# Summing the first 80 context row tiles on VectorE in runs of 16

## The reference

```python
sc = jnp.einsum('thsk,hsnk->thsn', qp, subkeys)             # scores against 2 x 128 keys, 8 heads
top_s, top_i = lax.top_k(sc, 16)
...
best_s, best_p = lax.top_k(cand_s, 16)                      # of 16 x 16 sums
expert = jnp.take_along_axis(cand_i, best_p, axis=-1)
g = jax.nn.softmax(best_s, axis=-1)
act = jax.nn.gelu(jnp.einsum('thkd,td->thk', u_tab[expert], xt))
return jnp.einsum('thk,thkd->td', g * act, v_tab[expert])
```

## Time and profile before

| | |
|---|---|
| median of 3 runs | 4857.98 us (4857.04 to 4867.78) |
| the profiled execution | 4852.7 us, span 4851.0 us |
| TensorE (PE) busy, whole span | 3834.6 us, 79% |
| VectorE (DVE) busy | 2912.3 us, 60% |
| ScalarE (ACT) busy | 1545.0 us, 32% |
| GpSimd (POOL) busy | 1622.4 us, 33% |
| chain that ended last | PE 43%, DMA 25%, DVE 20%, issue 6%, ACT 3% |

### The profile page before, as it was taken

One profiled execution on the slowest core, in us unless ns is written; L12 is line 12 of the kernel. 1 busy time (PEld: TensorE's weight loads), 2 busy tenths in 40 slices (PEclk: granted clock), 3 DMA queues, 4 the chain that ended last, 5 costly groups with the idle time before them and its releaser, 6 DMA issues.

```text
span 4851.0 us, 43978 instructions
## 1 busy us (share of the span) xinstructions
PE 3834.6 (79%) x11761; PEld 1564.1 (32%) x11761; DVE 2912.3 (60%) x6845; ACT 1545.0 (32%) x4811; POOL 1622.4 (33%) x1312
## 2 busy tenths in 40 slices
PE   6999898889999657999876669988876656666666
PEld 4645355554444212344322113344222211111110
DVE  1112588666576697454488885455568996544544
ACT  4111244332122233333333333233433433333333
POOL 0000133222232233333333334344333425555554
PEclk8999899999999867999977679999987766666666
DMA  6544788889999887999988989999999879999998
GB/s 256 217 182 184 252 313 294 308 296 356 361 411 372 328 333 282 380 380 380 402 347 348 392 322 400 422 384 398 413 390 385 335 291 366 410 421 414 414 421 353
DMA packets 290056, 1687.27 MB, mean 348 GB/s; under 512 B 29136, under 2 KB 71184, under 8 KB 111120
## 3 DMA queue, kind: packets, MB, share of 16 engines
q0 software_dynamic: 184320, 1342.26, 69.7%
q1 hardware_dynamic: 97472, 318.79, 17.4%
q10 hardware_dynamic: 8016, 23.42, 1.5%
HBM read 1646.57 MB, written 37.78 MB: 347 GB/s over the span
## 4 chain that ended last, share of the span: by engine, by line
PE 43%; DMA 25%; DVE 20%; issue 6%; ACT 3%; POOL 1%; SPq 1%; DVEq 0%; ACTq 0%; POOLq 0%
PE ps L1218 31%; DMA slots<-in_peer,idxR 20%; PE ps L1234 8%; DVE slots L1503 6%; POOL slots L959 1%; DVE gsmR L1582 1%; DMA ring<-in_wq 1%; DVE ti L1523 1%; DVE ti L1520 1%; DMA ring<-in_mlat 1%; DVE hot L1555 1%; DVE hot L1559 1%; DVE picked L1561 1%; DVE tv L1522 1%; ACT lhs L1010 1%
## 5 line engine op out<-in xcount | busy, mean ns | idle before, releaser
L959 POOL DMA_INDIRECT slots<-in_peer,idxR x1280 | 1616.0, 1263 | 3175.3 <-PE ps L1234 2042.6
L1234 PE MATMUL ps<-slots,lhs 128*64 128x512 f32 x4544 | 1523.5, 785 | 823.5 <-ACT lhs L1010 804.2
L1503 DVE CUSTOM_DVE_ANT_0 slots<-slots,h2R 128x1024 f32<-128x1024 f32 x1280 | 1543.1, 1224 | 670.9 <-issue 591.1
L1218 PE MATMUL ps<-ring,arena 128*128 128x512 f32 (+1 forms) x3996 | 1577.7, 552 | 42.0 <-DMA ring<-in_wq 22.7
L1218 PEld LDWEIGHTS ps<-ring,arena 128*128 128x128 f32 x3996 | 764.8, 195 | 872.8 <-issue 804.6
L1234 PEld LDWEIGHTS ps<-slots,lhs 128*64 128x64 f32 x4544 | 298.0, 161 | 1943.3 <-ACT lhs L1010 1678.5
L999 ACT ACTIVATE gelus<-dots 128x1 f32<-128x1 f32 x1280 | 256.1, 200 | 1651.7 <-DVE dots L1503 1640.1
L1010 ACT ACTIVATE lhs<-fold,wgts 128x64 f32<-128x64 f32 x1136 | 395.1, 348 | 37.1
L1002 ACT ACTIVATE wgts<-gelus,gsmR 128x1 f32<-128x1 f32 x1280 | 377.1, 295 | 42.5 <-ACT gelus L999 0.5
L1218 PE MATMUL ps<-ring,slots 128*128 128x512 f32 (+1 forms) x704 | 250.7, 518 | 0.0
L1515 DVE SCALAR_TENSOR_TENSOR slots<-slots,wgts 128x1024 f32<-128x1024 f32 x135 | 173.1, 1282 | 91.1 <-ACT wgts L1002 85.5
(11 more groups left out here) (198 smaller groups left out, 2380.0 us busy)
## 6 DMA issues: line engine op xcount, KB each, us to landing
ring<-in_whead SPq DMA_DIRECT2D x24, 2048.0 KB
ring<-in_wa SPq DMA_DIRECT2D x24, 2048.0 KB
ring<-in_wq SPq DMA_DIRECT2D x16, 2048.0 KB
slots<-in_peer,idxR POOLq DMA_INDIRECT x1280
ring<-in_wlate SPq DMA_DIRECT2D x16, 1024.0 KB
ring<-in_wgc SPq DMA_DIRECT2D x16, 1024.0 KB
ring<-in_wgb SPq DMA_DIRECT2D x8, 2048.0 KB
ring<-in_wout SPq DMA_DIRECT2D x8, 2048.0 KB
```

The source lines that it names most:

```text
L959: g.indirect_dma_start(out=slot(R), out_offset=None, in_=a["peer"], in_offset=bass.IndirectOffsetOnAxis(ap=idxR[:, p % KEEP, g2, col:col + ...
L1218: done = mm(out, lhsT, rhs, start=n == 0, stop=n == len(pairs) - 1)
L1234: done = mm(ps[j * HALF:(j + 1) * HALF, g2, :], weights, slot(R)[:, D + j * UW:D + (j + 1) * UW], start=start, stop=stop)
L1503: v.tensor_tensor_reduce(out=u, in0=u, in1=h2R[:, g2, :], scale=1.0, scalar=0.0, op0=ALU.mult, op1=ALU.add, accum_out=dots[:, R % LHS:R % ...
```

## The change

The condition that kept rows before the end of the context's ranking out of the chained rows goes. All runs of 16 from row 0 that end before the event `wq` of group 1 are chained: rows 0 to 223, fourteen runs in place of nine. The position of every row in the list, the slots, the gathers and everything else stay. For rows 0 to 79 the broadcast on ScalarE and the matmuls on TensorE go (but for rows 15, 31, 47, 63 and 79, which are multiplied with `fold`), and VectorE gets 5 scalings and 75 accumulations.

```diff
@@ merge
-        placed, first, last = [], None, None
+        placed, last = [], None
...
             if ev.kind == "wq" and ev.g == 1 and last is None:
                 last = n
             if ev.kind == "gsm" and ev.g == 0:
-                first = n
                 self.few = -(-(row + 1) // FEW) * FEW
...
-        self.chains(placed, first, last)
-
-    def chains(self, placed, first, last):
+        self.chains(placed, last)
+
+    def chains(self, placed, last):
 
         self.chained = set()
         for R in range(0, len(placed) - RUN, RUN):
-            if placed[R] >= first and placed[R + RUN - 1] < last:
+            if placed[R + RUN - 1] < last:
                 self.chained.update(range(R, R + RUN))
```

## The result

The changed kernel took 4902.8 us in the median of four runs beside 4861.8 us: a ratio of 1.0089 (95% interval 1.0065 to 1.0113), +41 us. Run again beside 4858.7 us it took 4913.5 us, ratio 1.0104 (1.0090 to 1.0119), +55 us by the medians and +50 by the ratio. It is slower, by 0.9 to 1.0%.

The account below looks back on a forecast made before the run. TensorE was taken to bound the projections by little; VectorE, given 100 us more, would bound the stretch. Gross +81 us less 15 for run-ahead made +66, a forecast median of 4924 us, range 4885 to 4970.

Parts of the forecast that it names:

- Projections: Heads 0 and 1, 53 rows: 66.4 us of new VectorE work, 8 us of it taken by idle time; +58 us.
- The beat check: Projections of heads 0 and 1: each tile's 9.79 us beat becomes 12.5; +43 us over sixteen tiles.
- Scans: Scans of heads 0 and 1: sixteen steps, each 1.08 us longer as in head 3; +17 us.
- My lower end: Scans of heads 0 and 1: 18 additions fill VectorE's 20.5 us wait for the scan's product; +3 us.
- The other nine rows: Rows 0 to 3 and 75 to 79: 11.0 us of VectorE work, half hidden; +6 us.
- The run-ahead: Behind row 79: TensorE, up to six tiles (42 us) ahead, lets evictions run faster; -15 us, ends 0 and 19.
- (a): VectorE at row R waits for the weight of row R-2: taken as 0, between 0 and 51 us.
- (b): Gather slots, six until row 84, are freed by the next row's addition: taken as 0, at most +20 us.
- Rival A: 560 to 914 us: VectorE's idle time swallows the additions, so the kernel gets faster, 4843 us; chance 0.06.
- Rival B: Nothing is hidden: the 100 us come whole and the run-ahead is lost in the scans, 4958 us; chance 0.12.
- Rival C: Half-idle TensorE gets a lower clock, lengthening matmuls in the scans' round trips: 4960 us; chance 0.10.
- The signs: Expected in the trace: 210 accumulations, row 79 about 80 us later, VectorE over 90% busy in projections, later shift 60 to 70.

Follow-up runs that it names:

- experiment 1: Kernel before, rows 0 to 79 still on TensorE, plus idle VectorE work as long as each addition, waiting for no engine: 4924.9 against 4856.0 us, ratio 1.0141.
- (2): Kernel before plus idle VectorE work for rows 0 to 79, one instruction of 512 columns a row: 4890.7 against 4857.3 us, ratio 1.0064.
- experiment 3: Changed kernel with additions of rows 0 to 79 over 128 of 1024 columns, all waits kept: 4852.5 against 4856.0 us (kernel before), ratio 0.9992.
- experiment 7: Kernel before with no chained rows at all, rows 80 to 223 on TensorE too: 4927.5 against 4857.3 us, ratio 1.0145.
- experiment 6: Kernel before with only the run of rows 64 to 79 chained more: 4854.4 against 4857.3 us, ratio 0.9996.
- experiment 4: Changed kernel without the five run-end matmuls of rows 15, 31, 47, 63, 79: 4899.4 against 4856.0 us (kernel before), ratio 1.0092.

## Why the prediction was right, and where its terms were off

The sign and its reason hold: VectorE's work of 254 us in 320 plus 100 us more is longer than the stretch, and it makes the loss: the work alone costs as much and more (experiment 1), half of it half (2), and with the work cut short and all waits kept the stage is as long as before (3). The forecast was 4924 us with +66, between 4885 and 4970; the medians were 4903 and 4914. The sum of terms, against the table:

- **Projections: +58 forecast, +54.5 measured.** Right: of 66.7 us of added work 12 were hidden, where I had said 8. The beat check (+43) was too low as it let all idle time be used.
- **Scans: +17 forecast, +4 measured.** This term was mis-sized. I took the step of head 3, where rows are chained, less that of head 0, where they aren't: 5.46 - 4.38 = 1.08 us. That compares two heads, not two ways. With no chained rows head 3's step is (1066.51 - 1033.43)/7 = 4.73 us (experiment 7), so chaining makes 0.73 there; in head 0 it makes (743.54 - 711.48)/7 - 4.38 = 0.20, in head 1 0.63 (5.17 in place of 4.54). My lower end (+3: the additions fill VectorE's wait for the scan's product) was the right reading, and that wait did fall from 20.5 to 8.0 us. Experiment 6 shows it alone, with +3.5 us in head 1.
- **The other nine rows: +6 forecast.** Not seen: the first query eviction of head 0 comes 0.4 us later, and head 2's part got shorter.
- **The run-ahead: -15 forecast.** Measured: head 2's projections -2.6 us, with rows 75 to 79 in them. The step that failed is "when the ranking ends it stands up to six tiles ahead, 42 us". It never does: the scans tie TensorE to VectorE step by step, so it leaves head 1's scans without a lead (909.3 us) and reaches row 79's run end 28 us later, where it waits 2.5 us. The long stands at run ends, 33.8, 20.3 and 41.8 us, lie in heads 0 and 1 and cost nothing. Without any run end head 2's projections take 972.8 - 916.5 = 56.3 us, 8.4 less than before (experiment 4), which is the time of the row matmuls that are gone from between the tiles; the run end of row 79 takes 5.8 of the 8.4 back.

So errors of opposite sign cancelled in part: the gross sum was 13 (scans), 6 (nine rows) and 3.5 us (projections) too high, and what comes back 12 too high: +66 against +57 in the trace. Head 2's scans, +1.3, had no term. That the number came so near is in part luck.

- **New waits.** (a) The wait for a weight: taken at nothing, measured 15.3 us in 560 to 980 us; experiment 3, which keeps it, loses nothing as a whole, and experiment 1, which has no such wait, loses more than the change. (b) The gather with six slots: taken at nothing; no such wait after.
- **Rival A** (faster) needs the idle time to take the additions. It takes 24 us of the first 55 and 10 of the next 47 (experiments 1 and 2): not enough. **Rival B** (nothing hidden, +100) is wrong by 43 us. The rule of the Trainium skill beside it (Perfetto Trace Analysis, Identifying the Most-Contended Engine) did better than I let it: by weight-load time (150.9 of 320 us) TensorE had headroom in the stretch, and taking 75 rows off it brought 11 us where VectorE's work stayed (experiment 1 against the change) and some 14 us outside the projections where it was cut short (experiment 3), of 77 us. A beat that is TensorE's to the hundredth shows who is last, not by how much.
- **Rival C** (the clock) happened where it costs little. The granted clock of the projections fell from 0.96 and 0.93 to 0.73, while TensorE stood at run ends; in the scans it was 1.00 and 0.92 against 1.00 before. The burst behind the wait of 33.8 us starts at the low level, 1.2 GHz (a granted clock of 0.50):

```profile
647.60:650.00 2.40, 2.34 (x5) 0.73 (x6) 2.40 (x5) 0.50 (x2) 1.18 (x1) 0.50 0.08 31
```

The picture of the Trainium skill (TensorE: Matmul & The Clock Gate, HAM oscillation), bursts that start at the low level, agrees with this row. Head 1's scans can carry little of it: in experiment 6 they grow by 3.5 us at a granted clock of 0.96, in the change by 3.7 at 0.92.
- **The signs.** Counts, VectorE's share (95 and 96%) and the steady shift behind 1000 us came as said. Row 79's dot comes at 932.0 in place of 869.1 us, 63 later and not 80. The projection beat is 13.6 us on average, just over the forecast 12 to 13, and the scan steps are 4.6 and 5.2 us, below the forecast 5.5.

## What to carry to other kernels

Where two engines share a stretch at 87 and 79%, moving work from the fuller to the other can cost most of its time. **Split the stretch by kind of work** and count the receiver's idle time in each part, not over the whole. In the projections, where VectorE was idle 24 of 191 us, 54.5 of the 66.7 us moved there came through; in the scans of heads 0 and 1, where it was idle 27 of 81 us beside round trips, 22.8 us cost 3.9. The same move paid where the giver was full, the receiver half idle and no gather stood in the chain of waits (group 2), so place it by stretches. And to price an instruction put into a loop step, compare that step with and without it, not two steps at different places.

## What the runs showed of the hardware

Relief of TensorE can be worth little while its timeline looks full: it was 87% busy with a beat of 9.79 us made wholly of its matmuls, and yet the change's relief of it shortened the stage by only 11 us against experiment 1 (448.0 to 437.1), of some 77 us of matmuls. Four run-end matmuls take 1.98 us behind a wait of 33.8 us, at a granted clock of 0.50, and 1.08 us in head 0's scans without a wait, at 1.00. And the DMA engines' busy share told little by itself: the same edit won 22 us at 96% and none at 99%, while in the chain of waits before gathers had no part in the one and 38% in the other.
